# Feed-forward weights in host-laid, partly interleaved blocks, in a three-stage fp32 transformer kernel

## Time and profile before

| what | value |
|---|---|
| median of 3 runs | 2057.83 us |
| profiled execution: its own time, from first to last instruction (span) | 2057.3 us |
| TensorE matmul busy | 2013.4 us, 98%, 10148 instructions |
| TensorE weight load busy | 1574.5 us, 77% |
| VectorE, ScalarE, GpSimd busy | 55%, 42%, 45% |
| from memory | 190.48 MB, 94 GB/s over the span |

### The profile page before, as it was taken

One profiled execution on the slowest core, in us unless ns is written; L12 is line 12 of the kernel. 1 busy time (PEld: TensorE's weight loads), 2 busy tenths in 40 slices (PEclk: granted clock), 3 DMA queues, 4 the chain that ended last, 5 costly groups with the idle time before them and its releaser, 6 DMA issues.

```text
span 2057.3 us, 26250 instructions
## 1 busy us (share of the span) xinstructions
PE 2013.4 (98%) x10148; PEld 1574.5 (77%) x10148; DVE 1135.5 (55%) x2020; ACT 867.9 (42%) x1381; POOL 917.4 (45%) x1157
## 2 busy tenths in 40 slices
PE   6999999999999999999999999999999999999998
PEld 2877676888888767768888888786776788888877
DVE  5366758988393579955522231466996543222235
ACT  4542434443233556784322222445578532222242
POOL 1344205876566325541555555302355155555540
PEclk9999999999999999999999999999999999999999
DMA  9034631322323211103333323322111332332331
GB/s 328 25 108 143 217 123 50 105 94 80 121 84 102 89 42 42 62 21 123 92 103 103 99 86 103 102 69 83 42 42 42 103 97 98 103 103 83 102 102 62
DMA packets 188299, 194.26 MB, mean 94 GB/s; under 512 B 8592, under 2 KB 184080, under 8 KB 187792
## 3 DMA queue, kind: packets, MB, share of 16 engines
q1 hardware_dynamic: 187600, 189.44, 28.5%
q10 hardware_dynamic: 576, 3.15, 0.4%
HBM read 190.48 MB, written 2.10 MB: 94 GB/s over the span
## 4 chain that ended last, share of the span: by engine, by line
PE 88%; DVE 6%; POOL 2%; ACT 2%; DMA 1%; issue 1%; SPq 0%; DVEq 0%; ACTq 0%; POOLq 0%
PE ps L808 20%; PE ps L810 20%; PE ps L809 20%; PE ps L827 3%; PE ps L829 3%; PE ps L828 3%; PE ps L855 2%; POOL wl L2900 1%; DVE mix L2512 1%; PE ps L844 1%; PE ps L845 1%; PE ps L846 1%; PE ps L1355 1%; PE ps L1428 1%; PE ps L1411 1%; PE ps L1374 1%
## 5 line engine op out<-in xcount | busy, mean ns | idle before, releaser
L2900 POOL TENSOR_TENSOR wl<-ring,wh 128x256 fp32r<-128x256 f32 x1008 | 754.2, 783 | 807.5 <-ACT wh L1465 807.2
L1465 ACT ACTIVATE wh<-ring 128x1024 fp32r<-128x1024 f32 (+1 forms) x298 | 309.0, 1044 | 311.1 <-PE ps L810 256.9
L808 PE MATMUL ps<-xh,wh 128*128 128x512 f32 (+1 forms) x976 | 383.1, 393 | 2.6 <-POOL wl L2900 2.6
L810 PE MATMUL ps<-xh,wl 128*128 128x512 f32 (+1 forms) x976 | 380.6, 390 | 0.0
L809 PE MATMUL ps<-xl,wh 128*128 128x512 f32 (+1 forms) x976 | 380.6, 390 | 0.0
L808 PE MATMUL ps<-acts,wh 128*128 128x512 f32 x880 | 343.5, 390 | 0.7 <-POOL wl L2900 0.4
L810 PE MATMUL ps<-acts,wl 128*128 128x512 f32 x880 | 342.4, 389 | 0.0
L809 PE MATMUL ps<-acts,wh 128*128 128x512 f32 x880 | 342.4, 389 | 0.0
L2512 DVE SCALAR_TENSOR_TENSOR mix<-ps,par,mix 128x441 f32<-128x441 f32 (+2 forms) x352 | 213.7, 687 | 29.3 <-ACT mix L1712 29.3
L808 PEld LDWEIGHTS ps<-xh,wh 128*128 128x128 f32 (+1 forms) x976 | 183.0, 188 | 47.0 <-issue 9.1
L810 PEld LDWEIGHTS ps<-xh,wl 128*128 128x128 f32 (+1 forms) x976 | 183.0, 187 | 39.4
(11 more groups left out here) (443 smaller groups left out, 3031.4 us busy)
## 6 DMA issues: line engine op xcount, KB each, us to landing
ring<-in_w_ff_dram SPq DMA_DIRECT2D x64, 1024.0 KB, 5.2
ring<-in_w_in_dram SPq DMA_DIRECT2D x28, 1024.0 KB, 5.0
ring<-in_ffn_w_up_dram SPq DMA_DIRECT2D x22, 1024.0 KB, 4.9
ring<-in_w_ada_dram SPq DMA_DIRECT2D x17, 1024.0 KB, 5.0
ring<-in_w_out_dram SPq DMA_DIRECT2D x12, 1024.0 KB, 5.1
ring<-in_ffn_w_down_dram SPq DMA_DIRECT2D x8, 1024.0 KB, 5.0
ring<-in_w_ple_gate_dram SPq DMA_DIRECT2D x8, 1024.0 KB, 5.0
early<-in_w_ada_dram SPq DMA_DIRECT2D x7, 1024.0 KB, 10.8
```

The lines of the kernel that those rows point to most:

```text
L808: t.matmul(b[0:m, 0:n], s.hi[:, k, a:a + m], x2[0][:, k, :], start=k == ks[0], stop=False)
L810: i = t.matmul(b[0:m, 0:n], s.lo[:, k, a:a + m], x2[0][:, k, :], start=False, stop=k == ks[-1])
L1465: a.activation(s.hi[:, :, c], s.ap[:, :, c], ACT.Copy).then_inc(*up("hi", "hi", name, hf))
L2900: i = p.tensor_tensor(s.lo[:, k:k + 2, c], s.ap[:, k:k + 2, c], s.hi[:, k:k + 2, c].bitcast(F32), ALU.subtract)
```

## The change

All feed-forward weights are laid out by the host: for each tile of 256 columns one block, in which a partition's 2048 numbers lie in one run, half by half, and within a half in groups of `step` row blocks. In a group the `step` row blocks are interleaved: the numbers of row blocks k to k + step - 1 for the same column are neighbours. So the stationary operand of a row block is read with a step of `step` elements (`held`). With step 1 it is contiguous as before. The table `STEP` sets it per group of products. A half is now one contiguous run of 1024 numbers (768 for the last down group), for the load, the copy and the subtraction. Where a tile with a step follows one without in the same slot of `wh`, or the reverse, each half overlaps both old halves, and `before` names both. The tiles `acts{l}0` and `acts{l}1` grow by 64 elements, and `U[0]` and `U[1]` begin 8 and 32 elements in (layer 0), 16 and 64 elements in (layer 1).

```diff
+STEP = {("ug", 0): 4, ("uv", 0): 4, ("ug", 1): 8, ("uv", 1): 8, ("ug", 2): 2, ("uv", 2): 2, ("dn", 0): 2, ("dn", 1): 4, ("dn", 2): 6,
+        ("ff1", 0, 0): 2, ("ff1", 0, 1): 2, ("ff1", 0, 2): 4, ("ff1", 0, 3): 4,
+        ("ff2", 0, 0): 2, ("ff2", 0, 1): 2, ("ff2", 0, 2): 4, ("ff2", 0, 3): 4,
+        ("ff1", 1, 0): 8, ("ff1", 1, 1): 8, ("ff1", 1, 2): 1, ("ff1", 1, 3): 2,
+        ("ff2", 1, 0): 8, ("ff2", 1, 1): 8, ("ff2", 1, 2): 2, ("ff2", 1, 3): 2}
...
+    def held(self, x, k, a, m=128):
+        if not self.step:
+            return x[:, k, a:a + m]
+        n = self.step
+        return x.rearrange("p (h q i n) -> p h q i n", h=2, i=128, n=n)[:, a // 128, k // n, :, k % n]
+    def half(self, x, hf):
+        if not self.step:
+            return x[:, :, 128 * hf:128 * hf + min(128, self.w - 128 * hf)]
+        return x[:, self.kt * 128 * hf:self.kt * 128 * (hf + 1)]
+    def quarters(self, x, hf):
+        x = self.half(x, hf)
+        return [x[:, k:k + 2, :] if not self.step else x[:, 128 * k:128 * k + 256] for k in range(0, self.kt, 2)]
...
         for name, hf in order:
-            slot = (self.named[name].at, hf)
-            self.before[name, hf] = held.get(slot)
-            held[slot] = (name, hf)
+            t = self.named[name]
+            old = [held[t.at, h] for h in range(2) if (t.at, h) in held]
+            self.before[name, hf] = [b for b in old if b[0] != name
+                                     and (b[1] == hf or (self.named[b[0]].step is None) != (t.step is None))]
+            held[t.at, hf] = (name, hf)
...
-            b = self.before[name, hf]
-            if b is not None and self.through[b][1] >= n:
+            if any(self.through[b][1] >= n for b in self.before[name, hf]):
                 return False
...
-                a0 = sb(f"acts{l}0", 8192, F32R, where=low)
+                a0 = sb(f"acts{l}0", 8256, F32R, where=low)
-                    a1 = sb(f"acts{l}1", 8192, F32R, where=high)
+                    a1 = sb(f"acts{l}1", 8256, F32R, where=high)
...
-            n.U = [[a[:, v * 4096:(v + 1) * 4096].rearrange("p (j t) -> p j t", j=8) for v in range(2)] for a in (a0, a1)]
+            n.U = [[a[:, o + v * 4096:o + (v + 1) * 4096].rearrange("p (j t) -> p j t", j=8) for v in range(2)]
+                   for a, o in zip((a0, a1), ((8, 32), (16, 64))[l])]
...
+                if s.step:
+                    d.dma_start(s.ap, s.srcs[0]).then_inc(*up(f"slot{s.i % NSLOT}", "load", s.name, by=16))
+                    return
...
-                    t.matmul(b[0:m, 0:n], s.hi[:, k, a:a + m], x2[0][:, k, :], start=k == ks[0], stop=False)
+                    t.matmul(b[0:m, 0:n], s.held(s.hi, k, a, m), x2[0][:, k, :], start=k == ks[0], stop=False)
...
-                if b is not None:
+                for b in W.before[name, hf]:
                     e.wait_ge(*done(W.through[b][0]))
-                c = W.columns(name, hf)
-                a.activation(s.hi[:, :, c], s.ap[:, :, c], ACT.Copy).then_inc(*up("hi", "hi", name, hf))
+                a.activation(s.half(s.hi, hf), s.half(s.ap, hf), ACT.Copy).then_inc(*up("hi", "hi", name, hf))
...
-                for k in range(0, s.kt, 2):
-                    i = p.tensor_tensor(s.lo[:, k:k + 2, c], s.ap[:, k:k + 2, c], s.hi[:, k:k + 2, c].bitcast(F32), ALU.subtract)
+                for lo, raw, hi in zip(*[s.quarters(x, hf) for x in (s.lo, s.ap, s.hi)]):
+                    i = p.tensor_tensor(lo, raw, hi.bitcast(F32), ALU.subtract)
...
+def blocks(w, step):
+    kt = w.shape[0] // 128
+    v = w.reshape(kt // step, step, 128, w.shape[1] // 256, 2, 128)
+    return v.transpose(3, 2, 4, 0, 5, 1).reshape(w.shape[1] // 256, 128, kt * 256)
```

More of the change, by code:

```diff
@@ L313, in __init__ @@
     def __init__(self, i, srcs, kt, w, split, own):
-        self.i, self.srcs, self.kt, self.w, self.split, self.own = i, srcs, kt, w, split, own
+        self.i, self.srcs, self.kt, self.w, self.split, self.own, self.step = i, srcs, kt, w, split, own, None
+    def held(self, x, k, a, m=128):
[10 more added lines that the diff above has]
+        return [x[:, k:k + 2, :] if not self.step else x[:, 128 * k:128 * k + 256] for k in range(0, self.kt, 2)]
 class Weights:
@@ L325, in restart, with add @@
         self.uses = []
-    def add(self, name, src, kt, w, split=True, own=False):
+    def add(self, name, src, kt, w, split=True, own=False, step=None):
         t = Tile(len(self.tiles), src if type(src) is list else [src], kt, w, split, own)
+        t.step = step
         t.at, t.name = self.n_split % 2, name
@@ L614, in ada_w, with laid @@
                 W.add(("ada", i), A["w_ada"][0, :, i * 256:i * 256 + 256], 8, 256, split=False)
-        def down_w(name, w, k0, kt):
-            for i in range(4):
-                W.add((*name, i), w[k0 * 128:(k0 + kt) * 128, i * 256:i * 256 + 256], kt, 256)
+        def laid(name, i, w, kt):
+            W.add((*name, i), w, kt, 256, step=STEP[name])
         ada_w(range(3, 4))
@@ L633, in build @@
                 for jp in range(GR[g] // 2):
-                    o = (sum(GR[:g]) // 2 + jp) * 256
-                    W.add(("ug", g, jp), w_up[:, FF1 + o:FF1 + o + 256], 8, 256)
-                    W.add(("uv", g, jp), w_up[:, o:o + 256], 8, 256)
-            else:
-                down_w(("dn", g), w_dn, sum(GR[:g]), GR[g])
+                    for what in ("ug", "uv"):
+                        laid((what, g), jp, A[f"{what}{g}"][jp], 8)
+            else:
+                for i in range(4):
+                    laid(("dn", g), i, A[f"dn{g}"][i], GR[g])
         for l in range(2):
@@ L649, in build @@
             for kind, g in (("u", 0), ("u", 1), ("d", 0), ("u", 2), ("d", 1), ("u", 3), ("d", 2), ("d", 3)):
[L650 to L653, removed]
+                what = "ff1" if kind == "u" else "ff2"
+                for i in range(4):
+                    laid((what, l, g), i, A[f"{what}{l}{g}"][i], 8)
             W.add(("ple", l), [A["w_ple_2"][l][:, q * 256:q * 256 + 256] for q in range(4)], 8, 256)
@@ L657, in build @@
             o = t.i % NSLOT * SLOT
-            t.ap = ring[:, o:o + t.kt * t.w].rearrange("p (k n) -> p k n", k=t.kt)
+            t.ap = ring[:, o:o + t.kt * t.w]
             o = t.at * SLOT
-            t.hi, t.lo = [x[:, o:o + t.kt * 256].rearrange("p (k n) -> p k n", k=t.kt) for x in (wh_t, wl_t)]
+            t.hi, t.lo = [x[:, o:o + t.kt * 256] for x in (wh_t, wl_t)]
+            if not t.step:
+                t.ap, t.hi, t.lo = [x.rearrange("p (k n) -> p k n", k=t.kt) for x in (t.ap, t.hi, t.lo)]
         mixer, layer = [{x: list(pieces(t)) for x, t in tab.items()} for tab in (MIXER, LAYER)]
@@ L2011, in low_half @@
             def low_half(name, hf):
-                s, c = W.named[name], W.columns(name, hf)
+                s = W.named[name]
                 e.wait_ge(*at("hi", name, hf))
-                v.tensor_tensor(s.lo[:, :, c], s.ap[:, :, c], s.hi[:, :, c].bitcast(F32),
-                                ALU.subtract).then_inc(*up("lo_vec", "lo", name, hf))
+                v.tensor_tensor(s.half(s.lo, hf), s.half(s.ap, hf), s.half(s.hi, hf).bitcast(F32), ALU.subtract).then_inc(*up("lo_vec", "lo", name, hf))
             def after():
@@ L3013, in _ @@
             gpsimd(Seat(eng), eng)
[L3016 to L3017 removed]
+_INS = ["w_ada", "w_in", "w_out", "w_in_2", "w_q_up_2", "w_iq_up_2", "w_out_2", "w_ple_gate_2", "w_ple_2"]
 def by_feature(a):
     return a.T.reshape(-1, 128, a.shape[0]).transpose(1, 0, 2)
+def blocks(w, step):
+    kt = w.shape[0] // 128
+    v = w.reshape(kt // step, step, 128, w.shape[1] // 256, 2, 128)
+    return v.transpose(3, 2, 4, 0, 5, 1).reshape(w.shape[1] // 256, 128, kt * 256)
 def laid_out(inputs):
     d = {name: inputs[name] for name in _INS}
+    up, dn = inputs["ffn_w_up"][0], inputs["ffn_w_down"][0]
+    for g in range(3):
+        a, b = 128 * sum(GR[:g]), 128 * sum(GR[:g + 1])
+        d[f"uv{g}"], d[f"ug{g}"] = blocks(up[:, a:b], STEP["uv", g]), blocks(up[:, FF1 + a:FF1 + b], STEP["ug", g])
+        d[f"dn{g}"] = blocks(dn[a:b], STEP["dn", g])
+    for l in range(2):
+        for g in range(4):
+            d[f"ff1{l}{g}"] = blocks(inputs["w_ff1_2"][l][:, 1024 * g:1024 * g + 1024], STEP["ff1", l, g])
+            d[f"ff2{l}{g}"] = blocks(inputs["w_ff2_2"][l][1024 * g:1024 * g + 1024], STEP["ff2", l, g])
     d["x"], d["ctx"] = by_feature(inputs["x"][0]), by_feature(inputs["ctx"][0])
```

20 lines of the change are left out of this document (9 added, 11 removed).

## The result

| | before | after |
|---|---|---|
| median (lowest to highest, runs) | 2057.53 us (2057.06 to 2060.84, 4) | 2108.64 us (2107.60 to 2109.71, 4) |
| span of the profiled execution | 2057.3 us | 2105.8 us |
| ratio of the times | | 1.0237, 95% interval 1.0224 to 1.0250 |

The change costs 51 us (48.5 between the two spans), where 0.5 was forecast. The time lies in the range given (2035 to 2150), on the side of the first rival.

A forecast was written before the change was run, and what follows sets the result against it. TensorE, busy 98% of 2057.3 us, was taken as the bound, through its matmul pace. All terms were 0 except +0.5 us for the waits, giving 2057.8, stated as 2058 us against the median; range 2035 to 2150 us.

The forecast's parts named there:

- the first rival: Every product with a step: the stream collides more, slower; +195 or +130 us, weak form +5 to +40; chance 0.22.
- (1): Weight loads read with a step, 2640 matmuls at 4 or more: taken as 0, upper end +281 us.
- the second rival: 2640 matmuls at step 4 or more: the load outruns its cover, slower; 2339 us at three times today's load; chance 0.08.
- (2): Moving stream beside the stepped weight load, 4656 feed-forward matmuls: taken as 0, bounds -54 to +195 us.
- (3): Feed-forward activations U[0] and U[1] at later addresses: only starts move, taken as 0, with the bounds of (2).
- (4): Conversions of weight halves on ACT, DVE and POOL: same number, under TensorE's time per product, taken as 0.
- (5): Six places where the layout changes, conversions wait for both old halves: +0.5 us for all six, upper bound 13 us.
- (6): 94 weight transfers from memory with longer rows, nearly all hidden behind matmuls: 0, at the lower end -3 us.
- The rival of faster times: Feed-forward products: collisions of load and stream go, faster; step 2 alone -21 us, all -54 us; chance 0.22.

The follow-up runs named there:

- 5: 80 groups of 20 equal matmuls with 64 to 512 moving columns and steps 1 to 16, added at the end of the kernel before; 233.4 ns at step 4, 256 columns.
- the sweep: 88 groups of 20 equal fp32r matmuls, varying starts, steps and column counts, added behind the last product of the kernel before; 226.6 to 240.0 ns by starts alone.

## Why the prediction was wrong

The time lies in the range, but the forecast, 2058 us and no change, failed, and so did the reasons for it. That the range held is in part luck: its upper end was drawn for prices of 130 us and more, and none of them came. The 51 us are two rivals together, each in a small form, and the prediction's own sign of being wrong (one group of steps more than 1 ns off 226.7) came in every group with a step. An estimate from the loads alone in 5 (6.7 ns over 226.7 at step 4, 11 and up to all of 17.5 at step 8): 22 to 29 of the 46 us are the load's own length, the rest of the steps and the 3.4 us without a step are what is called collision here.

By its steps:

(1) **The load with a step: failed.** I bounded it rightly, said that cover is gone at 2.04 times today's 111 ns, and took 0 because the cover was larger than the whole stream. Measured: 233.4 ns at step 4, 2.1 times, and 219 to 267 at 6 to 16. It passes the cover of 226.7 by 7 ns at step 4 and by 11 to 20 at step 8, and hardly or not at all at step 6 (223 to 229). That is the second rival in its smallest form; I gave it 0.08 and priced only three times. The sign to look for was given as "near 299 ns with the end unmoved": the loads show 309 and the end moved. Uniform step 4 costs 37 us over the blocks at step 1 and step 8 costs 77.

The Trainium skill, "Advanced Engine Details and Errata", section "SBUF Cachelines", was the warning. Its rule (two accesses to a line of 16 bytes hide the latency, a new line each time costs) agrees in kind: 120 ns or less at steps 1 and 2, 233 at 4. It gives no size, and does not foresee that step 12 (266.7) costs more than 4 and step 16 (220.0) less.

(2) **The stream beside the load: failed**, and is the first rival in its weak form. Step 2 was free by (1), and still pays 6.6 ns (233.3), with the load well under cover; step 6 pays 9.4 ns, most of it in this way. Another page of the Trainium skill, "TensorE: Matmul & The Clock Gate", section "Step-by-step: what each phase is for", says that loading the next weights takes no read bandwidth from the running matmul; the rows here differ (226.6 to 240.0 ns by the starts alone, 233.4 when only the weights' start moves by 8 elements), and the measurement decides. The bounds held: -11.7 to +40 ns at steps 2 and 4. The choice of 0 rested on recorded durations at the end of a run, which are modelled, and on the means of the earlier trace rows.

(3) **Activations further on: failed.** 0 was taken because `xh` and `acts` at other addresses differ by 2 ns. But by the sizes of the tiles both start at whole multiples of 512 bytes from the weights' starts in the kernel before (a tile's second half begins 512 bytes into its rows), so the comparison never varied what matters. Measured: 8 to 9 us alone, 3.5 beside the steps; 6.6 ns at 32 bytes, 2.2 at 64 bytes, 0 at 256 and 512.

(4) **The conversions: held.** L1490 1.05 us, L2039 1.22, L2924 0.78, as before.

(5) **Waits for both halves: the mechanism was there, in another place and larger.** Not a wait for `wl`, but the evacuation queued behind the late copies on ScalarE, 1.4 us at 310 us in place of 0.5 for all six places. No new wait of TensorE is seen at the other five places in the run with the blocks alone.

(6) **The transfers: held.** Pieces fall from 188299 to 101515, landings from 5.2 to 4.8 us, for nothing on the path:

```profile
ring<-in_ff_dram SPq DMA_DIRECT2D x64, 1024.0 KB, 4.8
```

With (1), (2), (3) and (5) at their measured sizes the sum is 2057.3 + 46.1 (steps) + 3.4 (products without a step over moved starts) + 1.4 = 2108.2, against a span of 2105.8. For the two layers it fits: 33.2 us by it, 33.3 measured. The 2.4 us lie before and in the first block, and are the net of four: 1.6 less had passed by 32 us, before any changed product (the first product of L912 starts at 31.80 us before and its counterpart at 30.18 after); the dip of the clock behind the wait at 343 us adds 1.6; three short waits for `wl`, 0.9 us, are gone; and the first products of the up projection, which wait for the norm, pay 0.2 us until 343 us in place of 0.9. About 0.8 us stay open.

The rival of faster times (collisions go) was half right: starts and steps do move the pace. But no start and no step tried went below the old layout's 226.7 ns; the 8 ns that went with a moving operand standing still are out of reach for a real product.

## What to carry to other kernels

In fp32r products of 512 columns, let the stationary operand be contiguous and let weights and activations start as far apart as here or a whole number of 256 bytes more; another start costs up to 13 ns of 227 per matmul, a step of 2 to 8 elements 7 to 18. A load that seems to have half of a matmul as cover loses all or nearly all of it once each column comes from another group of four elements (219 to 267 ns against 226.7). Before calling an address or a stride free, ask whether the kernel at hand has ever varied it.

## What the runs showed of the hardware

- The distance of two fp32r matmuls of 512 columns is 226.7 ns at best, 13.3 more than their columns at 2.4 a nanosecond. Many groups of the sweep stand at exactly 226.7, 233.3 or 240.0 ns in the mean; others lie between (228.9 at a shift of 3 elements, without alternating), and why is open.
- With contiguous weights a shift of the moving operand by 7 elements is free (226.6) and one of 5 is the worst (240.0); 256, 768 and 1024 bytes are free. 512 bytes cost 1.0 ns in the sweep when the moving operand shifts and nothing when the weights do, and nothing in the whole kernel (226.7). Why is open.
- A load of 128 fp32r columns takes 0.87 ns per column at step 1, at most 0.94 at 2, 1.35 at 3, 1.82 at 4, 1.86 to 1.93 at 8, 2.08 at 12, 1.72 at 16. The last value, below that of step 4, is not explained.
- A moving operand of 512 columns with a step of 2 elements takes 451 ns per matmul, twice as long, with contiguous weights.
- Under plain fp32 matmuls of two passes (429.2 ns) neither steps up to 8 nor loads of 314 ns cost anything: the load has twice the cover. Other starts were not tried there.
